# Six pairs of feature tiles of the down projection by seven block products each, in two phases, with the gate on the accumulators

## What is computed

```
gf, uf = jnp.split(h @ w_ffn_up[l], 2, axis=-1)
gf = causal_dwconv(gf, w_ffn_conv[l], b_ffn_conv[l])
y_ffn = (jax.nn.gelu(gf, approximate=True) * uf) @ w_ffn_down[l]
x = x + gate2[:, None, :] * y_ffn
...
return modulate(rmsnorm(x, g_final), shift_f, scale_f)
```

## Time and profile before

| | |
|---|---|
| timed runs, median of 3 | 961.87 us (961.83 to 962.41) |
| profiled execution, span | 960.0 us |
| timed median less that span | 1.87 us |
| PE busy | 949.8 us, 99% of the span |
| DVE busy | 633.6 us, 66% |
| ACT busy | 415.0 us, 43% |
| the down stage on PE | first matmul starts at 822.67 us, last at 953.01 us |

### The profile page before, as it was taken

How to read it: one execution, slowest core, us unless ns; L and a number is a source line. 1 busy time by engine, 2 the same in 40 slices (tenths; PEclk the granted TensorE clock), 3 DMA queues, 4 the chain that set the end, 5 groups by cost and what they waited for, 6 DMA issues and landing times.

```text
span 960.0 us, 12336 instructions
## 1 busy us (share of the span) xinstructions
PE 949.8 (99%) x4662; PEld 803.8 (84%) x4662; DVE 633.6 (66%) x856; ACT 415.0 (43%) x548; POOL 10.3 (1%) x33
## 2 busy tenths in 40 slices
PE   8999999999999999999999999999999999999997
PEld 8788888888988888989888898888888888888885
DVE  4889998522578787854678447776764345756845
ACT  6679777222246263454424464223222232422511
POOL 0120000000000000000000000000000000000000
PEclk9999999999999999999999999999999999999999
DMA  9753312336555536332236504656533422252101
GB/s 331 256 154 99 98 44 72 98 98 211 179 155 173 183 115 203 115 104 74 88 129 222 175 23 143 208 178 206 184 94 118 161 87 87 91 215 89 44 23 66
DMA packets 106287, 129.43 MB, mean 135 GB/s; under 512 B 5260, under 2 KB 81796, under 8 KB 106124
## 3 DMA queue, kind: packets, MB, share of 16 engines
q1 hardware_dynamic: 105864, 128.38, 40.7%
q10 hardware_dynamic: 388, 0.58, 0.2%
HBM read 126.81 MB, written 2.14 MB: 134 GB/s over the span
## 4 chain that ended last, share of the span: by engine, by line
PE 97%; DVE 1%; ACT 1%; issue 0%; POOL 0%; DVEq 0%; POOLq 0%; ACTq 0%
PE ps L1778 31%; PE ps L1780 31%; PE ps L1779 31%; PE ps L1845 1%; PE ps L2038 1%; DVE ada_acc L1117 1%; PE ps L1865 0%; PE ps L2167 0%; PE ps L1828 0%; ACT htmp L727 0%; DVE wsplit L1242 0%; PE ps L1837 0%; ACT h L730 0%; ACT wsplit L722 0%; DVE o_nat L1770 0%
## 5 line engine op out<-in xcount | busy, mean ns | idle before, releaser
L1778 PE MATMUL ps<-h,wsplit 128*128 128x512 f32 (+1 forms) x816 | 312.1, 383 | 0.0
L1780 PE MATMUL ps<-h,wsplit 128*128 128x512 f32 (+1 forms) x816 | 310.8, 381 | 0.0
L1779 PE MATMUL ps<-h,wsplit 128*128 128x512 f32 (+1 forms) x816 | 310.7, 381 | 0.0
L1094 DVE TENSOR_TENSOR wsplit<-wraw,wsplit 128x2048 fp32r<-128x2048 f32 (+2 forms) x78 | 164.7, 2112 | 93.4 <-ACT wsplit L681 61.8
L1780 PEld LDWEIGHTS ps<-h,wsplit 128*128 128x128 f32 x816 | 153.4, 188 | 29.6
L1778 PEld LDWEIGHTS ps<-h,wsplit 128*128 128x128 f32 x816 | 153.5, 188 | 28.8 <-issue 0.2
L1779 PEld LDWEIGHTS ps<-h,wsplit 128*128 128x128 f32 x816 | 153.5, 188 | 28.5
L681 ACT ACTIVATE wsplit<-wraw 128x2048 fp32r<-128x2048 f32 (+2 forms) x68 | 119.0, 1750 | 101.8 <-PE ps L1780 101.4
L1712 DVE SCALAR_TENSOR_TENSOR cv<-ps,vec,cv 128x511 f32<-128x511 f32 (+1 forms) x48 | 35.9, 748 | 53.8 <-ACT cv L1049 50.7
L1151 DVE SCALAR_TENSOR_TENSOR ada_acc<-ada_raw,small,ada_acc 128x512 f32<-128x512 f32 x84 | 63.1, 751 | 2.8
L1778 PE MATMUL ps<-wsplit,act_s 128*128 128x512 f32 x160 | 62.2, 389 | 0.0
(11 more groups left out here) (258 smaller groups left out, 1387.9 us busy)
## 6 DMA issues: line engine op xcount, KB each, us to landing
wraw<-in_w_ffn_up SPq DMA_DIRECT2D x24, 1024.0 KB, 5.1
wraw<-in_w_in SPq DMA_DIRECT2D x23, 1024.0 KB, 5.3
ada_raw<-in_w_ada SPq DMA_DIRECT2D x16, 1024.0 KB, 7.1
wraw<-in_w_ffn_down SPq DMA_DIRECT2D x10, 1024.0 KB, 4.9
ada_raw<-in_w_ada_final SPq DMA_DIRECT2D x8, 1024.0 KB, 5.1
ada_first<-in_w_ada SPq DMA_DIRECT2D x7, 1024.0 KB, 11.8
wraw<-in_w_in SPq DMA_DIRECT2D x12, 512.0 KB, 3.9
wraw<-in_w_proj_rnn SPq DMA_DIRECT2D x8, 640.0 KB, 4.3
```

Of the source, the lines that this page charges most:

```text
L1094: ve.tensor_tensor(wsplit[:, s, LO, 0:n], wraw[:, s, 0:n], wsplit[:, s, HI, 0:n].bitcast(F), ALU.subtract).then_inc(w_lo, 1)
L1778: te.matmul(dst, lhs(LO), rhs(HI), start=start, stop=False)
L1779: te.matmul(dst, lhs(HI), rhs(LO), start=False, stop=False)
L1780: return te.matmul(dst, lhs(HI), rhs(HI), start=False, stop=stop)
```

## The change

Two neighbouring tiles and two halves of the tokens (256 each), two tiles and two halves of the columns (512 each) are two 2 x 2 block matrices. For six pairs of tiles, features 0 to 11 of 24, their product is no longer made from eight block products but from seven, of sums and differences of blocks (Strassen's scheme in Winograd's form). A block product is 2 token blocks x 3 = 6 matmuls of 512 columns. The four results are sums of these products, some with products in common.

- **First phase** (`first_products`, six chunks): four products of each pair, 24 matmuls. DVE makes three sums of 512 columns of the weights in place (`weight_sums`) where it multiplied by the gate; ACT keeps a copy of one of them (`t_kept`, 512 columns) ahead of the high part. Three differences of 256 tokens of the activations (`token_sums`) are made by DVE, for pairs 0 to 3 in the up stage and for pairs 4 and 5 between the chunks of this phase.
- **Between the phases** (`cross_terms`) DVE copies and combines PSUM banks with eight operations of 512 columns into `cross`; PE goes on summing in banks 0, 2, 4, 6, 1 and 3.
- **Second phase** (`second_products`, six chunks): the other three products of each pair, 18 matmuls. The odd tile of weights is loaded again (512 KB), DVE makes one sum (`weight_last`) and one difference (`token_last`, 256 tokens); the high and low parts are of 1536 columns of weights and of 512 + 256 tokens.
- **Plain chunks** (four in the ring and the two extra ones) are multiplied as before, without the gate on the weights. Ahead of them `base` adds the gated `cross` rows to the residual: six times two dependent DVE operations of 512 columns. ACT waits for all of them (`cross_done` 20) before it makes the first extra chunk's high part, since `act_x` lies in the memory of `cross`.
- **Tail**: the gate now multiplies each finished bank, one more DVE operation for each bank (eight in all).

The loops of the down stage are written out on all engines, and so is DVE's loop over up steps 7 to 10. The core of the diff:

```diff
-            def down_hi(c0, i=0):
-                s = c0 % 2
-                ae.wait_ge(w_gated, c0 - C_DOWN + 1 + 2 * i)
...
+            def first_hi(j):
+                c0 = C_DOWN + j
                 s = c0 % 2
+                ae.wait_ge(t_sum, 3 * j + 3)
+                ae.wait_ge(w_used, c0 + 1)
+                ae.activation(t_kept[j][:, :], wraw[:, s, 3 * T:4 * T], ACT.Copy)
                 ae.activation(wsplit[:, s, HI], wraw[:, s], ACT.Copy).then_inc(w_hi, 1)
+                ae.wait_ge(s_sum, 3 * j + 3)
+                down_act_hi(c0, 0, T, act[:, 2 * j])
+                down_act_hi(c0, 1, T, pair_sum[:, j % 4].rearrange("p a n -> p (a n)"))
...
             def down_hi_x(n):
-                ae.wait_ge(wx_gated, n + 1)
+                ae.wait_ge(wx_loaded[n], 16)
+                ae.wait_ge(cross_done, 20)
...
+            for j in range(1, NS):
+                first_hi(j)
+            for j in range(NS):
+                second_hi(j)
+            plain_hi(C_PLAIN)
             down_hi_x(0)
-            down_hi(C_END - 2)
+            plain_hi(C_PLAIN + 1)
             down_hi_x(1)
...
+            def weight_sums(j):
...
+                ve.wait_ge(w_loaded[s], landed(c0))
+                ve.tensor_tensor(w[2], w[1], w[3], ALU.add).then_inc(t_sum, 1)
+                ve.tensor_tensor(w[1], w[0], w[1], ALU.add).then_inc(t_sum, 1)
+                ve.wait_ge(t_sum, 3 * j + 2)
+                ve.tensor_tensor(w[3], w[1], w[3], ALU.add).then_inc(t_sum, 1)
...
             def first_down(i):
-                gate_down(C_DOWN)
-                down_lo(C_DOWN)
+                weight_sums(0)
+                first_lo(0)
             up_step(NF // 2 - 1, first_down)
...
+            weight_sums(1)
+            for j in range(1, NS):
+                first_lo(j)
+                if j + 3 < NS:
+                    token_sums(j + 3)
+                if j + 1 < NS:
+                    weight_sums(j + 1)
+            weight_last(0)
+            token_last(0)
+            second_lo(0)
+            weight_last(1)
+            token_last(1)
+            cross_terms()
+            for j in range(1, NS):
+                second_lo(j)
+                if j + 1 < NS:
+                    weight_last(j + 1)
+                    token_last(j + 1)
+            plain_lo(C_PLAIN)
+            for n in range(6):
+                base(n)
             down_lo_x(0)
+            plain_lo(C_PLAIN + 1)
...
-                    ve.tensor_tensor(x2[:, b, cs], ps[:, n, :], x1_nat[:, b, cs], ALU.add).then_inc(x2_add, 1)
-                    ve.wait_ge(x2_add, n + 1)
+                    ve.wait_ge(down_mm, n + 3)
+                    ve.tensor_tensor(x2[:, b, cs], ps[:, n, :], bc[:, 0, cs], ALU.mult).then_inc(x2_add, 1)
+                    ve.wait_ge(x2_add, 2 * n + 1)
+                    ve.tensor_tensor(x2[:, b, cs], x2[:, b, cs], x1_nat[:, b, cs], ALU.add).then_inc(x2_add, 1)
...
+            def first_products(j):
...
+                product(c0, 0, 256, 3, 5, begin, end)
+                if not end:
+                    product(c0, 1, 256, 2, 4, begin)
+                if begin:
+                    te.wait_ge(act_done, NF)
+                p1 = product(c0, 0, 0, 0, 0, begin, end)
...
+                product(c0, 1, 0, 1, 1, begin, end).then_inc(w_used, 1)
...
+            def second_products(j):
...
+                if j == 0:
+                    te.wait_ge(cross_done, 4)
+                product(c0, 0, 0, 0, 0, False)
+                if j == 0:
+                    te.wait_ge(cross_done, 6)
+                product(c0, 0, 256, 2, 4, False)
+                if j == 0:
+                    te.wait_ge(cross_done, 8)
+                product(c0, 1, 0, 1, 1, False).then_inc(w_used, 1)
```

More of the change, by code:

```diff
@@ L158, in hybrid_block @@
         act_x = at("act_x", 144, [P, 4, 2, T], F32R)
+        pair_sum = at("pair_sum", 152, [P, 4, 2, 256])
+        base_row = at("base_row", 152, [P, 2, T])
+        cross = at("cross", 144, [P, 2, 2, T])
+        t_kept = [at(f"t_kept{j}", 176 if j == 0 else 198 if j == 1 else 12 + 2 * j, [P, T]) for j in range(NS)]
         bc = at("bc", 178, [P, 3, D])
@@ new lines, in weight_last, with down_act_lo @@
+            def weight_last(j):
+                c0 = C_SECOND + j
+                s = c0 % 2
+                ve.wait_ge(w_loaded[s], landed(c0))
+                ve.wait_ge(w_hi, C_DOWN + j + 1)
+                ve.tensor_tensor(wraw[:, s, 2 * T:3 * T], t_kept[j][:, :], wraw[:, s, 0:T], ALU.add).then_inc(t_sum, 1)
+            def down_act_lo(c0, u, n, src):
+                sl = 2 * (c0 % 2) + u
+                ve.wait_ge(act_hi, 2 * (c0 - C_DOWN) + u + 1)
+                ve.tensor_tensor(act_s[:, sl, LO, 0:n], src, act_s[:, sl, HI, 0:n].bitcast(F), ALU.subtract)\
+                  .then_inc(act_lo, 1)
@@ new lines, in cross_terms @@
+            def cross_terms():
+                for a in range(2):
+                    ve.wait_ge(down_mm, 1)
+                    ve.tensor_copy(cross[:, 0, a], ps[:, 5 + 2 * a, :]).then_inc(cross_done, 1)
+                for a in range(2):
+                    ve.wait_ge(cross_done, a + 1)
+                    ve.tensor_tensor(cross[:, 0, a], cross[:, 0, a], ps[:, 2 * a, :], ALU.subtract)\
+                      .then_inc(cross_done, 1)
+                for a in range(2):
+                    ve.wait_ge(down_mm, 2)
+                    ve.wait_ge(cross_done, a + 3)
+                    ve.tensor_tensor(cross[:, 1, a], cross[:, 0, a], ps[:, 4 + 2 * a, :], ALU.subtract)\
+                      .then_inc(cross_done, 1)
+                for a in range(2):
+                    ve.wait_ge(w_used, whole(C_SECOND - 1))
+                    ve.wait_ge(cross_done, a + 5)
+                    ve.tensor_tensor(cross[:, 1, a], cross[:, 1, a], ps[:, 1 + 2 * a, :], ALU.add)\
+                      .then_inc(cross_done, 1)
@@ new lines, in base @@
+            def base(n):
+                which, half, op = ((0, 1, ALU.add), (0, 0, ALU.subtract), (1, 1, ALU.add))[n // 2]
+                a = n % 2
+                b = a + (0 if n < 2 else 2)
+                row = cross[:, which, a]
+                cs = slice(T * half, T * half + T)
+                ve.tensor_tensor(base_row[:, a], row, bc[:, 0, cs], ALU.mult).then_inc(cross_done, 1)
+                ve.wait_ge(cross_done, 9 + 2 * n)
+                ve.tensor_tensor(x1_nat[:, b, cs], x1_nat[:, b, cs], base_row[:, a], op).then_inc(cross_done, 1)
@@ L1729, in _ @@
             ada_biased(7, 6, ada_bias, 64)
-            with ve.Fori(7, NF // 2 - 1) as i:
+            for i in range(7, NF // 2 - 1):
                 up_step(i, lambda i: lo(C_UP + 2, i))
+                token_sums(i - 7)
             ve.wait_ge(bc_loaded, 16)
@@ L2217, in down_half @@
                 return mm3(ps[:, 2 * b + half, :], lambda part: act_s[:, 2 * s + u, part, P * b:P * b + P],
[L2218 to L2222, removed]
-                for u in range(2):
[L2224 to L2228, removed]
+                           lambda part: wsplit[:, s, part, D * u + T * half:D * u + T * half + T], start, stop, True)
@@ new lines, in product @@
+            def product(c0, u, col, q, bank, start, stop=False):
+                s = c0 % 2
+                for a in range(2):
+                    at_ = col + P * a
+                    ins = mm3(ps[:, bank + 2 * a, :], lambda part: act_s[:, 2 * s + u, part, at_:at_ + P],
+                              lambda part: wsplit[:, s, part, T * q:T * q + T], start, stop, c0 >= C_SECOND)
+                return ins
+            def first_products(j):
+                c0 = C_DOWN + j
+                begin, end = j == 0, j == NS - 1
+                te.wait_ge(w_lo, whole(c0))
+                te.wait_ge(act_lo, 2 * j + 2)
+                if begin:
+                    te.wait_ge(ada_out, 7)
+                product(c0, 0, 256, 3, 5, begin, end)
+                if not end:
+                    product(c0, 1, 256, 2, 4, begin)
+                if begin:
+                    te.wait_ge(act_done, NF)
+                p1 = product(c0, 0, 0, 0, 0, begin, end)
+                if end:
+                    p1.then_inc(down_mm, 1)
+                    product(c0, 1, 256, 2, 4, begin, end).then_inc(down_mm, 1)
+                product(c0, 1, 0, 1, 1, begin, end).then_inc(w_used, 1)
@@ L2229, in down_chunk, with plain_chunk @@
+            def plain_chunk(c0):
+                te.wait_ge(w_lo, whole(c0))
+                te.wait_ge(act_lo, 2 * (c0 - C_DOWN) + 2)
+                for u in range(2):
+                    for b in range(NB):
                         for half in range(2):
-                            ins = down_half(c0 % 2, u, b, half, start and u == 0, False)
+                            fresh = c0 == C_PLAIN and u == 0 and b >= 2 and half == 1
+                            ins = down_half(c0 % 2, u, b, half, fresh, False)
@@ L2231, in down_chunk @@
                 ins.then_inc(w_used, 1)
```

(6 more changed lines are left out.)

155 lines of the change are left out of this document (84 added, 71 removed).

## The result

The changed kernel takes 986.91 us (median of 4 runs, 986.02 to 987.43), the kernel before 961.85: ratio 1.0259, 95% interval 1.0245 to 1.0274. It is slower by 25 us, where 986.6 was forecast. The profiled execution has a span of 984.9 us (984.7 forecast), mean granted clock 0.987.

What follows compares the result with a forecast made beforehand. PE bound the kernel before; DVE and ACT rounds would now make it wait. Waits of 29.5 us, less 8.16, plus 0.72, 1.3 (load), 1.4 (clock) give span 984.7; with 1.87 to the timed median 986.6 us, range 982.5 to 992.

Steps and rivals of the forecast that it cites:

- Matmuls (8.16 us): On PE, six pairs need 42 matmuls each for 48, at 0.2267 us each: 8.16 us saved.
- First phase (15.8 us): First phase: PE needs 5.44 us a chunk, the DVE and ACT round 7.95 or 9.08; five waits, together 15.8 us.
- Between the phases and second phase (6.9 us): PE waits 2.80 us for cross operations, 0.97 for the next chunk, then four times 0.78 in rounds of 4.87.
- Plain chunks (6.8 us): PE waits 0.84 us before the first plain chunk and 6.0 before the second, behind `base` and the extra chunk.
- Tail (0.72 us): After the last bank, one more dependent DVE operation: 0.72 us added.
- The load (1.3 us): First plain chunk's load, slowed by two extra loads right behind it: costs 1.3 to 3.4 us, 1.3 taken.
- The clock (1.4 us): After the wait of 6.0 us before the second plain chunk, PE's clock falls to half: 1.4 us, an estimate.
- The claim that the slow clock costs nothing in the first phase: First phase: a slower PE costs nothing while a chunk at mixed speed fits in the round of 8 to 9 us.
- The rival that it would stay down through both phases: PE's clock stays at 1.2 GHz through first and second phase: about 1017 us; chance 0.07.
- The range: Whole kernel: 982.5 to 992 us, for 8 in 10, from the sum without load and clock to longer hops, later load, clock.

Runs made afterwards that it cites:

- The reordered kernel: Changed kernel, seven products kept, their preparation on ACT and DVE reordered and cut in smaller pieces: 958.53 us, ratio 0.9963 to the kernel before.
- ACT's order alone: Changed kernel with, on ACT only, the second plain chunk's high part ahead of the first extra chunk's: 986.28 us, ratio 1.0254 to the kernel before.
- The filled wait: Changed kernel with 23 matrix products of zeros filling PE's wait before the second plain chunk: 984.75 us, ratio 1.0234 to the kernel before.
- both orders moved: Changed kernel with the second plain chunk ahead of the first extra chunk on ACT and on DVE: 979.07 us, ratio 1.0174 to the kernel before.

## Why the prediction was right

- **Matmuls (8.16 us).** 4626 records for 4662, 0.2267 us each at full clock. Right. The reordered kernel keeps 3.4 us of it in its time: its stage is 4.24 us shorter than before (the other 3.9 went to the waits and restarts that are left), less the tail's 0.7.
- **First phase (15.8 us).** The round is 7.93 us for 7.95 forecast, with token sums 842.28 - 833.16 = 9.12 for 9.08. The waits of the third and fifth chunk are shorter than forecast (2.0 and 1.0 us from start to start, less a matmul) because a slow clock had stretched the chunk before by 1.7 and 1.5 us; the starts of PE are where the round puts them: 832.18, 841.31, 850.44, 858.37, 866.30, each 0.6 to 0.7 later than forecast, 0.48 of it from the start of the stage.
- **Between the phases and second phase (6.9 us).** DVE's cross operations end at 876.7 (876.2 forecast), rounds are 4.85 us (4.87). PE's wait before the second phase is 0.9 us and not 2.8, because the slow clock had stretched this last chunk too, by 1.7; it starts at 874.47, again 0.6 behind the forecast. So PE waited less than forecast (24.0 us in gaps from start to start, less a matmul each, for 29.5) and worked longer, and DVE set the same starts. Right in the starts.
- **Plain chunks (6.8 us).** The gap of 6.17 is 5.94 more than a matmul; 6.0 forecast. The prediction told this wait along ACT's queue and along DVE's order at once. ACT's order alone changed nothing: DVE's written order (`base`, extra chunk, plain chunk) was enough to cause the wait, and moving the chunk on both engines took it away.
- **Tail (0.72 us).** From the last matmul's start to the end 984.9 - 977.2 = 7.7, for 960.0 - 953.0 = 7.0 before. Right.
- **The load (1.3 us).** Wrong: nothing. The load was issued at 892.97 and landed after 4.9 us, as alone, although the two extra loads were issued right behind it; those took 8.1 and 10.2. ACT's high part of the first plain chunk starts at 898.49, released by PE. The row taken as nearest (6.4 us) was that of another load with one behind it; here the two behind did not slow this one.
- **The clock (1.4 us).** Nine intervals take 924.97 - 920.99 = 3.98 us, 2.04 at full rate: 1.9 us. The filled wait measured 1.5 to 2.2. The estimate was short because it took 2.8 us for the rise and the rise took 3.98. The claim that the slow clock costs nothing in the first phase was tested and holds. The Trainium skill (TensorE: Matmul & The Clock Gate, Part 1: The HAM clock gate) has half rate as the default that activity releases, and the rows of the down stage agree: each fall is behind a wait, and the rise comes within the chunk. The rival that it would stay down through both phases did not come about.
- **What made the sum hit.** The mechanism was right; that the total came within 0.3 us is in part luck. From the first to the last matmul start of the stage: 154.05 us for 130.34 before, +23.7; forecast +24.0. The load's 1.3 too much is made up by 0.5 of clock and restarts that cost more than taken: from DVE's end to PE's first matmul 0.14 us (832.04 to 832.18), and the second matmul follows after 0.31. The 0.48 us by which the stage begins later are there at 47 us already (a DVE operation at 47.12 that was at 46.64 before). In that stretch the change only makes one semaphore of two and leaves the work as it was. The clock fits: from 20 to 30 us it is 0.83 in this profile and 1.00 in the one before, and in the two experiments on the order of the plain chunks, with 1.00 there, the second chunk starts 0.4 and 0.6 us earlier (831.79 and 831.57 for 832.18). The four runs of the kernel differ by 1.4 us among themselves.
- **The range.** The prediction calls its lower bound, 982.5, the sum without the load and the clock (983.9) "and some tenths less"; it is 1.4 us less. Nothing hung on it.

## What to carry to other kernels

Fewer matmuls give nothing if their operands come from a chain of engines that takes longer than the matmuls: judge by the round (the time from one chunk's sums to the next chunk's), not by the busy share (DVE was at 66%). Write the round down as DVE's part, ACT's part and DVE's part again, compare it with what PE needs for a chunk, and where it is longer, cut the operations in pieces that follow each other closely and move independent work into the gaps; DVE's sum of work, 5.5 us here, is the bound, not the chain's 7.9. Look at each engine's written order for long helpers (`base`) ahead of what the critical engine needs next, and move them on all engines that they touch; moving them on ACT alone changed nothing, on ACT and DVE it took 7 us off.

## What the runs showed of the hardware

- The clock did not fall in each wait of the same length, and not always within the wait. Before the last chunk of the first phase PE's gap is 2.6 us in the changed kernel and with both orders moved (2.61 and 2.59); the granted clock from 866 to 873 us is 0.76 in the first and 1.00 in the second. In the profile of the changed kernel this chunk starts at full rate and is slow from its fourth matmul on (a start every 0.43 us from 867.10 to 870.08):

```profile
866.30 0.47 PE L1886 MATMUL ps<-wsplit,act_s 128*128 128x512 f32 x1 [2.22 <-DVE act_s L1747]
866.61 0.40 PE L1887 MATMUL ps<-wsplit,act_s 128*128 128x512 f32 x1
...
867.52 0.63 PE L1887 MATMUL ps<-wsplit,act_s 128*128 128x512 f32 x1
867.95 0.63 PE L1888 MATMUL ps<-wsplit,act_s 128*128 128x512 f32 x1
```

- A product of 128 x 128 float32 blocks is two matmul records and 0.22 us (42 products, 84 records, from 915.48 to 924.77), about as long as one matmul of 512 columns in the 32-bit format of the main products (0.23).
- Three independent pieces of 512 columns take 2.00 us on DVE, where one operation of 1536 columns took 1.76 in the changed kernel: each further piece costs 0.12 us. That is far less than the 2.50 us a round that DVE stood idle for ACT.
